# Sliding-window heads of a two-block layer stack: values stationary in two column strips, probabilities divided on ScalarE before the transpose, output born transposed; gain rows fetched by one transfer

## The reference

```python
def swa_sink_branch(q_in, k_in, v_in, positions, sinks):   # 16 query heads, 2 key/value heads of 64
    ...
    scores = jnp.einsum('bnqhgd,bnkhd->bnhgqk', qb, kw) * (SW_HEAD_DIM ** -0.5)
    ...   # causal, window of 128
    m = jnp.maximum(jnp.max(scores, axis=-1, keepdims=True), sink)
    p = jnp.exp(scores - m)
    probs = p / (jnp.sum(p, axis=-1, keepdims=True) + jnp.exp(sink - m))
    o = jnp.einsum('bnhgqk,bnkhd->bnqhgd', probs.astype(vw.dtype), vw)
    return o.reshape(B, S, SW_Q_W)

def hybrid_layer_2(...):
    h = rmsnorm(x, pre_mix_g)
    proj = h @ w_in
    y_a = deltanet_branch(...) @ w_up_dn
    y_b = swa_sink_branch(...) @ w_up_sw
    mix = (jax.nn.sigmoid(gate_a) * y_a + jax.nn.sigmoid(gate_b) * y_b) @ w_o
    x = x + rmsnorm(mix, post_mix_g)
    h2 = rmsnorm(x, pre_mlp_g)
    ff = jnp.square(jax.nn.relu(h2 @ w_ff1)) @ w_ff2
    return x + rmsnorm(ff, post_mlp_g)
```

## Time and profile before

| | |
|---|---|
| median of 3 runs | 1726.27 us (1726.08 to 1726.99) |
| the profiled execution's own time | 1726.3 us |
| its span, first to last instruction | 1724.5 us |
| PE / PEld busy | 1703.7 us (99%) / 1402.1 us (81%) |
| DVE / ACT / POOL busy | 1173.0 us (68%) / 915.6 us (53%) / 236.9 us (14%) |
| chain that ended last, by engine | PE 91%, DVE 3%, ACT 3%, issue 2%, POOL 1% |
| DMA | 270.10 MB, mean 157 GB/s |

### The profile page before, as it was taken

How to read it: one execution, slowest core, us unless ns; L and a number is a source line. 1 busy time by engine, 2 the same in 40 slices (tenths; PEclk the granted TensorE clock), 3 DMA queues, 4 the chain that set the end, 5 groups by cost and what they waited for, 6 DMA issues and landing times.

```text
span 1724.5 us, 28208 instructions
## 1 busy us (share of the span) xinstructions
PE 1703.7 (99%) x10753; PEld 1402.1 (81%) x10753; DVE 1173.0 (68%) x2216; ACT 915.6 (53%) x1666; POOL 236.9 (14%) x350
## 2 busy tenths in 40 slices
PE   9999999999999999999999999999999999999998
PEld 7878887888788788888787778888888787778887
DVE  5656667766556676768877775556778877766665
ACT  5345376453553754656646455445666545455553
POOL 1201200022012000143203000000233203000000
PEclk9999999999999999999999999999999999999999
DMA  8544444554435344643423445554633333455552
GB/s 293 172 150 137 163 137 147 195 196 157 164 123 171 124 164 166 198 165 103 131 90 124 147 158 184 196 195 148 223 120 123 123 99 104 163 173 184 183 183 88
DMA packets 137134, 270.10 MB, mean 157 GB/s; under 512 B 5549, under 2 KB 8745, under 8 KB 137001
## 3 DMA queue, kind: packets, MB, share of 16 engines
q1 hardware_dynamic: 134928, 265.44, 45.8%
q10 hardware_dynamic: 2072, 2.86, 0.5%
HBM read 267.23 MB, written 1.05 MB: 156 GB/s over the span
## 4 chain that ended last, share of the span: by engine, by line
PE 91%; DVE 3%; ACT 3%; issue 2%; POOL 1%; DMA 0%; ACTq 0%; DVEq 0%; POOLq 0%
PE bank L421 23%; PE bank L423 22%; PE bank L422 22%; PE bank L402 5%; PE bank L445 3%; PE bank L404 3%; PE bank L1687 1%; DVE lo L384 1%; PE bank L607 1%; PE bank L1664 1%; PE bank L1591 1%; PE bank L1630 1%; PE bank L1599 0%; PE bank L413 0%; PE bank L411 0%
## 5 line engine op out<-in xcount | busy, mean ns | idle before, releaser
L421 PE MATMUL bank<-hi,xhl 128*128 128x512 f32 (+1 forms) x1792 | 724.4, 404 | 2.4 <-DVE lo L384 1.5
L423 PE MATMUL bank<-hi,xhl 128*128 128x512 f32 (+1 forms) x1792 | 698.3, 390 | 0.0
L422 PE MATMUL bank<-lo,xhl 128*128 128x512 f32 (+1 forms) x1792 | 696.0, 388 | 0.0
L384 DVE TENSOR_TENSOR lo<-raw,hi 128x1024 fp32r<-128x1024 f32 (+1 forms) x504 | 611.8, 1233 | 48.0 <-PE bank L423 38.0
L374 ACT ACTIVATE hi<-raw 128x1024 fp32r<-128x1024 f32 (+1 forms) x504 | 519.5, 1050 | 234.5 <-PE bank L423 216.1
L421 PEld LDWEIGHTS bank<-hi,xhl 128*128 128x128 f32 x1792 | 337.1, 188 | 77.1 <-issue 13.8
L423 PEld LDWEIGHTS bank<-hi,xhl 128*128 128x128 f32 x1792 | 336.4, 188 | 72.9
L422 PEld LDWEIGHTS bank<-lo,xhl 128*128 128x128 f32 x1792 | 337.7, 188 | 59.8
L402 PE MATMUL bank<-xhl,hi 128*128 128x512 f32 x384 | 136.0, 398 | 0.0
L404 PE MATMUL bank<-xhl,lo 128*128 128x256 f32 x384 | 107.8, 281 | 0.0
L402 PEld LDWEIGHTS bank<-xhl,hi 128*128 128x128 f32 x384 | 72.1, 188 | 17.8
(11 more groups left out here) (316 smaller groups left out, 1890.1 us busy)
## 6 DMA issues: line engine op xcount, KB each, us to landing
raw<-in_w_in SPq DMA_DIRECT2D x135, 1024.0 KB, 5.1
raw<-in_w_ff SPq DMA_DIRECT2D x64, 1024.0 KB, 5.3
raw<-in_w_proj_a SPq DMA_DIRECT2D x8, 1024.0 KB, 5.1
raw<-in_w_proj_b SPq DMA_DIRECT2D x8, 1024.0 KB, 5.0
raw<-in_w_out SPq DMA_DIRECT2D x8, 1024.0 KB, 5.3
raw<-in_w_up_sw SPq DMA_DIRECT2D x8, 1024.0 KB, 5.0
raw<-in_w_up_dn SPq DMA_DIRECT2D x8, 1024.0 KB, 5.0
raw<-in_w_o SPq DMA_DIRECT2D x8, 1024.0 KB, 5.0
```

What stands on the lines that cost most here:

```text
L384: dve.tensor_tensor(self.lo[g % LO_RING][:, 0:w], src, self.hi[g % HI_RING][:, 0:w].bitcast(F32), ALU.subtract).then_inc(self.lo_ready, 1)
L421: pe.matmul(out, xh[:, row, t], self.hi[slot % HI_RING][:, w], start=first, stop=False)
L422: pe.matmul(out, xh[:, row, t], self.lo[slot % LO_RING][:, w], start=False, stop=False)
L423: mm = pe.matmul(out, xl[:, row, t], self.hi[slot % HI_RING][:, w], start=False, stop=last)
```

## The change

1. The steps of the sliding heads come from a new function, `sliding`. A new step `s_norm` follows `s_scores` (and `s_out`) in the same group: DVE takes the reciprocal there, and ACT multiplies the probabilities by it in place, in two instructions, before they are transposed. `s_turn` on PE now waits for this.
2. `s_out` works on two heads at once, in every other group. The values (128x64) are stationary, one head in the lower 64 columns of the array and one in the upper, and the turned probabilities move (256 columns, then 128). The result is the transposed output of two heads, 128x256. ACT copies it to `xh[1]`, DVE makes `xl[1]`. There are three `turned` buffers for two.
3. The four ("turn", "ys", n) steps of each layer are gone, and `ys` with them.
4. The squares of `dk` use bank OUT for bank TURN.
5. The gain rows are put into one array by the host, and ACT loads them by one transfer for five. The steps at the start are turn, turn, warm 10, for turn, warm 5, turn, warm 3.

```diff
+def sliding(heads):
+    out = []
+    for t in range(heads + 2):
+        out.append(([("s_turn", t - 1)] if 1 <= t <= heads else [])
+                   + ([("s_scores", t)] if t < heads else [])
+                   + ([("s_out", (t - 3) // 2)] if t >= 3 and t % 2 else [])
+                   + ([("s_norm", t)] if t < heads else []))
+    return out
...
-        p.steps += [("turn", "h", 0), ("warm", 5), ("turn", "h", 1), ("warm", 3)]
+        p.steps += [("turn", "h", 0), ("turn", "h", 1), ("warm", 10)]
...
-        for l in range(DEPTH):
-            act.dma_start(rows[l * R:l * R + KB, :], ins["norm_w"][l].rearrange("(k p) -> k p", p=P))\
-               .then_inc(*up("rows_loaded", (l, 0), 16))
-            act.dma_start(rows[l * R + KB:l * R + R, :], ins["subln_w"][l:l + 1, :])\
-               .then_inc(*up("rows_loaded", (l, 1), 16))
-        act.dma_start(rows[DEPTH * R:DEPTH * R + KB, :], ins["final_norm_w"].rearrange("(k p) -> k p", p=P))\
-           .then_inc(*up("rows_loaded", (DEPTH, 0), 16))
+        act.dma_start(rows[0:DEPTH * R + KB, :], ins["gain_rows"]).then_inc(*up("rows_loaded", 0, 16))
...
-    work = [[w for kind in ("s_turn", "s_scores", "s_out") for w in group if w[0] == kind] for group in attention("s", HEADS)]
+    work = sliding(HEADS)
...
-SQUARES_BANK = {"dk": TURN, "dq": OUT}
+SQUARES_BANK = {"dk": OUT, "dq": OUT}
...
                 if kind == "s_turn":
                     h = arg
                     core.free(pe, TURN)
-                    pe.wait_ge(*at("s_prob", h))
+                    pe.wait_ge(*at("s_scaled", h))
...
                 if kind == "s_out":
-                    h = arg
                     core.free(pe, OUT)
-                    pe.wait_ge(*at("s_copied", h))
-                    v = slice(HD * (h // (HEADS // 2)), HD * (h // (HEADS // 2)) + HD)
-                    pe.matmul(B[OUT][:, 0:HD], turned[h % 2][:, 0:P], vs[:, 0, v], start=True, stop=True)
-                    pe.matmul(B[OUT][:, HD:2 * HD], turned[h % 2][:, P:2 * P], vs[:, 0, v], start=True, stop=False)
-                    pe.matmul(B[OUT][:, HD:2 * HD], turned[h % 2][:, 2 * P:3 * P], vs[:, 1, v],
-                              start=False, stop=True).then_inc(*up("s_summed", h))
-                    core.hold(s, OUT, "ys", h)
+                    pe.wait_ge(*at("s_copied", 2 * arg + 1))
+                    strips = [(slice(HD * m, HD * m + HD), turned[(2 * arg + m) % 3]) for m in range(2)]
+                    k = 2 * arg // (HEADS // 2)
+                    v = slice(HD * k, HD * k + HD)
+                    for r, p in strips:
+                        pe.matmul(B[OUT][r, 0:S], vs[:, 0, v], p[:, 0:2 * P], start=True, stop=False, skip_group_check=True)
+                    for r, p in strips:
+                        mm = pe.matmul(B[OUT][r, P:S], vs[:, 1, v], p[:, 2 * P:3 * P], start=False, stop=True,
+                                       skip_group_check=True)
+                    mm.then_inc(*up("s_summed", arg))
+                    core.hold(s, OUT, "cut", ("ys", arg))
...
+                if kind == "s_norm":
+                    h = arg
+                    act.wait_ge(*at("s_inverse", h))
+                    for tb, first in ((0, 0), (1, P + 1)):
+                        part = prob[h % 2][:, first:first + (tb + 1) * P]
+                        ins_ = act.activation(part, part, ACT.Copy, scale=t1.inverse[:, h % 4, tb:tb + 1])
+                    ins_.then_inc(*up("s_scaled", h))
+                if kind == "s_out":
+                    act.wait_ge(*at("s_summed", arg))
+                    act.activation(core.xh[1][:, arg, :], B[OUT][:, 0:S], ACT.Copy).then_inc(*up("high", ("ys", arg)))
...
-                if kind == "s_turn":
+                if kind == "s_norm":
                     h = arg
                     dve.wait_ge(*at("s_prob", h))
                     dve.reciprocal(t1.inverse[:, h % 4, :], t1.total[:, h % 4, :]).then_inc(*up("s_inverse", h))
                 if kind == "s_out":
-                    h = arg
-                    dve.wait_ge(*at("s_summed", h))
-                    dve.wait_ge(*at("s_inverse", h))
-                    dve.tensor_tensor(ys[:, :, h * HD:h * HD + HD],
-                                      B[OUT][:, 0:2 * HD].rearrange("p (t d) -> p t d", t=TB),
-                                      bcast(t1.inverse[:, h % 4, :], 2, HD), ALU.mult).then_inc(*up("ys", h))
+                    dve.wait_ge(*at("high", ("ys", arg)))
+                    dve.tensor_tensor(core.xl[1][:, arg, :], B[OUT][:, 0:S], core.xh[1][:, arg, :].bitcast(F32),
+                                      ALU.subtract).then_inc(*up("cut", ("ys", arg)))
```

More of the change, by code:

```diff
@@ L1035, in _ @@
         pe.wait_ge(*at("ident_loaded"))
-        pe.wait_ge(*at("rows_loaded", (DEPTH, 0)))
+        pe.wait_ge(*at("rows_loaded"))
         pe.transpose(core.bank[SCORE[0]][:, 0:DEPTH * R + KB], rows[0:DEPTH * R + KB, :],
@@ L1177, in delta_slots @@
     put(21, ("silu", "dv"))
-    for at, name, n in ((1, "dv", 0), (9, "dv", 1), (11, "dv", 2), (17, "dv", 3), (21, "kd", 0), (27, "ys", 0),
-                        (25, "v", 0), (29, "ys", 1), (26, "v", 1), (29, "v", 2), (31, "v", 3), (42, "ys", 2),
-                        (43, "ys", 3), (45, "kd", 1), (55, "yd", 0), (57, "yd", 1), (61, "yd", 2)):
+    for at, name, n in ((1, "dv", 0), (9, "dv", 1), (11, "dv", 2), (17, "dv", 3), (21, "kd", 0), (25, "v", 0),
+                        (26, "v", 1), (29, "v", 2), (31, "v", 3), (45, "kd", 1), (55, "yd", 0), (57, "yd", 1), (61, "yd", 2)):
         put(at, ("turn", name, n))
@@ L1339, in block_two @@
     k_dec = flat8[:, 0:1024].rearrange("p (h d) -> p h d", d=P)
-    source = {"sq": b0, "sk": k_dup, "dq": b0, "dk": b1, "dv": b1, "ys": ys, "yd": vb,
-              "mix": qs}
-    xt_of = {"ys": 1, "yd": 0, "mix": 1}
-    half_of = {"ys": 1.0, "mix": 0.5}
+    source = {"sq": b0, "sk": k_dup, "dq": b0, "dk": b1, "dv": b1, "yd": vb, "mix": qs}
+    xt_of = {"yd": 0, "mix": 1}
+    half_of = {"mix": 0.5}
     tap = lambda j, n: 2 * KB + 1 + j * 3 * DHEADS + n
@@ L1351, in block_two @@
     with_sink = [(0, slice(0, P + 1)), (1, slice(P + 1, wide_tile))]
-    turned = [scr[:, 2304 + i * 384:2304 + (i + 1) * 384] for i in range(2)]
+    turned = [scr[:, 1544 + i * 384:1544 + (i + 1) * 384] for i in range(3)]
     junk = scr[:, 3072:4096]
@@ L1438, in _ @@
                     if n == 0:
-                        ready = {"us0": ("cut", ("ys", 3))}.get(job.name)
+                        ready = {"us0": ("cut", ("ys", HEADS // 2 - 1))}.get(job.name)
                         if ready:
@@ L1506, in _ @@
                             "dq": ("conv_in", "dq1"), "dk": ("conv_in", "dk1"), "dv": ("conv_in", "dv1"),
-                            "ys": ("ys", HEADS - 1), "yd": ("yd_gated", f), "mix": ("mix", f // 2),
+                            "yd": ("yd_gated", f), "mix": ("mix", f // 2),
                             "v": ("activated", ("silu", "dv")), "kd": ("silu", ("dk", 3))}.get(arg) or ("evac", f"up{arg[1:]}")
@@ L1901, in _ @@
                     act.wait_ge(*at("s_turned", h))
-                    if h >= 2:
-                        act.wait_ge(*at("s_summed", h - 2))
-                    act.activation(turned[h % 2], B[TURN][:, 0:3 * P], ACT.Copy).then_inc(*up("s_copied", h))
+                    if h >= 3:
+                        act.wait_ge(*at("s_summed", (h - 3) // 2))
+                    act.activation(turned[h % 3], B[TURN][:, 0:3 * P], ACT.Copy).then_inc(*up("s_copied", h))
+                if kind == "s_norm":
[8 more added lines that the diff above has]
+                    act.activation(core.xh[1][:, arg, :], B[OUT][:, 0:S], ACT.Copy).then_inc(*up("high", ("ys", arg)))
                 if kind == "decays":
@@ L2436 @@
     arrays.update(shape_constants())
+    norm_rows, head_rows = arrays.pop("norm_w").reshape(DEPTH, KB, P), arrays.pop("subln_w").reshape(DEPTH, 1, P)
+    gain_rows = np.concatenate([norm_rows, head_rows], 1).reshape(-1, P)
+    arrays["gain_rows"] = np.concatenate([gain_rows, arrays["final_norm_w"].reshape(KB, P)], 0)
     def program(tally):
```

## The result

The changed kernel takes 1756.83 us (median of 4 runs, 1755.80 to 1757.47), the kernel before 1726.17 (1725.92 to 1726.99). The ratio is 1.0176, interval 1.0164 to 1.0188: 30.7 us more. The forecast was 1743.4 with a range from 1731 to 1757. The direction and the loop through DVE and ACT came as forecast, and the size was 13.4 us short: the time lies inside the range by 0.2 us, and above the 1751 at which the main case ended.

What follows compares the result with a forecast made beforehand. The prediction took PE as the bound before and a DVE-ACT loop in the sliding heads after the change: 1726.3 + 22.4 (heads, two layers) - 3.3 (`ys` transposes) - 2.0 (start) = 1743.4 us, range 1731 to 1757.

Steps and rivals of the forecast that it cites:

- the loop through DVE and ACT: Sliding heads: DVE waits for ACT's exponential and output copy, so a period of two heads takes 10.5 us against 8.95.
- the main case: The case that the loop through DVE and ACT binds in the sliding heads: 1734 to 1751 us, chance 0.70.
- The start: Kernel start: one gain-row transfer for five lets the first chain begin 1.9 us earlier; -2.0 us, bounds -2.3 and 0.
- Head 15: Last sliding head: exponential delayed behind head 14's wait, PE's transpose 7.6 us after head 14's reciprocal; +2.1 us a layer.
- The clock: Rival: PE's new 2 us waits lower the clock; half of 14 costing 1.7 us gives 1756, up to 1768; chance 0.10.
- The `ys` transposes: Eight steps of four PE transposes gone, 0.41 us each: -3.3 us in all, bounds -4.0 and -2.0.
- The strips: Output product of a head pair on PE, two strips side by side: 0.89 us for 1.31, bounds 0.74 and 1.31.
- The other sign: Rival: DVE's waits in the heads stay under 0.8 us, PE decides, each pair saves 0.42 us; 1714.3 us, chance 0.12.
- A shorter loop: Rival: earlier output copy on ACT makes the period 9.9 us, head 15 costs nothing; 1732, at best 1727; chance 0.08.

Runs made afterwards that it cites:

- e1: The kernel before with only the new start (one transfer of gain rows; order turn, turn, warm 10): 1724.06 us.
- e5: The changed kernel with POOL's two silu operations cut from 128x512 to 128x1, leaving that multiply out: 1750.28 us.
- e6: The changed kernel with added 128x128 products keeping PE busy in its waits before even heads' and head 15's turns and the gates' second bank: 1752.75 us.
- e10: e9 with the division left out (no reciprocal, no multiplies, output not divided): 1717.24 us.
- e8: e7 plus the output's high-part copy ahead of the odd head's exponential on ACT and head 15's sink columns ahead of POOL's power operations: 1740.49 us.
- e7: The changed kernel with a head's maximum moved ahead of the split before it, on DVE alone: 1746.32 us.
- e9: e8 plus even heads' sink columns ahead of the silu on POOL: 1727.51 us.
- e2: The kernel before with only the division moved (s_norm behind each s_scores), outputs still per head and copied: 1753.86 us.
- e3: The changed kernel with the division left out (no s_norm, output not divided): 1731.93 us.
- e12: e9 with the odd heads' reciprocal on DVE moved behind the first two operations of the convolution: 1726.50 us.
- e11: The changed kernel with only POOL's order moved: even heads' sink columns ahead of the silu, head 15's ahead of the power operations: 1748.15 us.
- e4: The changed kernel with the whole division one group later (turn of head t-2, scores of t, division of t-1): 1737.36 us.

## Why the prediction came out short

The time lies in the range by 0.2 us, and that is luck: the upper end was widened for the clock, which accounts for some 4 us, while the split (6.6 us in both layers) and the wait for the bank (4.2) had no case of their own.

- **The start**: -2.0 forecast, -2.3 measured (e1). Right, within its bounds.
- **The loop through DVE and ACT**: 10.5 a period forecast, 11.1 measured, 10.35 without POOL's silu (e5). Every wait was at its place with its size; the term that was mis-sized is the split, 1.14 to 1.21 us in the working and 1.75 to 2.00 in one of two splits per period. This is 3.3 us a layer.
- **Head 15**: +2.1 and the turn at 7.6 us after the reciprocal were right (7.58). The sentence behind it failed, a term put at nothing: what DVE is late beyond PE there, "about 1.5, I count as hidden behind ACT's work of the delta rule". It is not hidden: the convolution holds the bank of the very next product, 2.09 us.
- **The clock**: the rival had the mechanism and the price of one stretch (1.7). It took half of 14 waits for costly; three stretches a layer came and one cost. 2.0 us a layer (e6) instead of 6. Its time of 1756 is met, but not by its sum. The prediction had also called itself wrong if the clock fell during the heads. By that sign it failed: two of the three stretches of a layer lie in the heads.
- **The sum**: the three missing terms, 3.3 + 2.1 + 2.0 = 7.4 a layer, stand against 7.0 missing in H (18.2 on average for 11.2). They are not quite additive, since e6's added products stand in the bank's wait too.
- **The `ys` transposes**: -1.64 a layer forecast, -1.42 measured. **The strips**: 0.89 forecast, 0.80 measured. The Trainium skill (TensorEngine Tiling (Array Packing), Key Properties) has a drain at a change of tiling mode, by which the pair was put near 1.31; the trace doesn't bear that size out, 0.80 lies near the lower bound of 0.74.
- **The other sign** (1714.3 if the waits are hidden): e10, where there is no division to wait for, gives 1717.2, so even that rival's gain was 3 us too large. With the division ahead of the turn, no order tried went below 1726.5.
- **A shorter loop**: this rival held that an earlier output copy on ACT would take 0.6 off the period. The queue as written didn't do it, and e8, which moves the copy ahead, has the period of e7 (10.7), since POOL's columns hold it there. What the earlier copy gives in e9 wasn't separated.

The cause of the loss is settled as far as e2, e9 and e10 go: the division between exponential and turn costs 27.5 us in the old order of the queues (e2; in the kernel with strips 24.9, against e3) and 10.3 in e9's. What the last 10.3 consist of is read from e9's trace (turn waits 2.1 a layer, bank waits 2.6, ACT fuller), not shown by an experiment.

## What to carry to other kernels

When a step is put between a producer and its consumer, price its place in each in-order queue, not its duration: 0.80 us of multiplies a head cost 24.9 us in the changed kernel (against e3), and 10.3 after other steps had been moved ahead on three engines (e9 against e10). After each wait that is removed, look for the next row that ended last (maximum, then POOL's sink columns, 0.18 us each but 1.18 beside a split, then the split); a cheap step on an engine that is busy for 14% of the time held ACT, DVE and PE. And when an engine becomes late, check what it will then run beside, and which bank it still holds.

## What the runs showed of the hardware

**DVE and POOL hold each other up.** The split L395 reads two SBUF operands. Beside POOL's two-operand product its length grows with the overlap: overlap 0.25 us, 1.33 long (e9); 0.83, 1.91 (e12); 0.92, 2.00 (changed kernel); without it 1.22. So beyond the first 0.14 us, DVE makes no progress until POOL's operation ends. The convolution L2053, which reads PSUM and one SBUF operand, takes 2.68 us beside POOL's L2347 (778.29) and the first 0.4 us of L2349 (779.87), and 2.68 with POOL idle (835.41). The Trainium skill (SBUF — State Buffer, Who interferes with whom) says that a DVE instruction with two SBUF inputs contends with a GpSimd instruction that reads SBUF, that the shared ports are an exclusive lock, and that issue order decides who blocks. The trace agrees, in both directions: in e8 POOL's first sink column, issued while the split runs, takes 1.18 us of the four copies' 1.54.

**The lower clock came behind waits of PE, but no length of a wait decides it in these runs.** In the changed kernel's first layer the stretches at 1.2 GHz begin in the turn after 1.90 us of idle time (at 763.08), in the one after 2.31 (807.46), and with the product after 2.09. But at 785.12 PE had idled 2.31 too, and kept 2.4 GHz. Shorter waits were followed by a fall as well: 1.70 and 1.65 us in e11's second layer, and in e4's two close together, 1.18 and 0.71 (fall at 1348.2), which passed without one in its first layer (828.43, 829.66). e9, e10 and e12, with no wait over 1.42 us in the heads, have none there.
